# Finer steps in the norm chain, query projections packed to full tiles, and another order of copies for the latents, keys and values of the third mixer

## The reference

```python
def rmsnorm_2(x, g):
    xf = x.astype(jnp.float32)
    y = xf * lax.rsqrt(jnp.mean(xf * xf, axis=-1, keepdims=True) + RMS_EPS)
    return (y * g.astype(jnp.float32)).astype(x.dtype)
...
def mla_mixer(h, positions, w_in, q_norm_g, w_uq, kv_norm_g, w_ukv, w_o):
    q_a, kv_a, k_rope = jnp.split(h @ w_in, [Q_LORA, Q_LORA + KV_LORA], axis=-1)
    q = (rmsnorm_2(q_a, q_norm_g) @ w_uq).reshape(bsz, L, MLA_HEADS, QK_NOPE + QK_ROPE)
    q_nope, q_rope = q[..., :QK_NOPE], q[..., QK_NOPE:]
    kv = (rmsnorm_2(kv_a, kv_norm_g) @ w_ukv).reshape(bsz, L, MLA_HEADS, QK_NOPE + V_DIM)
    k_nope, v = kv[..., :QK_NOPE], kv[..., QK_NOPE:]
    q_rope = apply_rope(q_rope, cos[:, :, None], sin[:, :, None])
    k_rope = apply_rope(k_rope, cos, sin)
...
    return o @ w_o
```

## Time and profile before

| | |
|---|---|
| median of 3 runs | 1678.65 us (1676.46 to 1680.81) |
| profiled execution | 1677.19 us, span 1675.5 us, mean granted clock 0.994 |
| PE busy | 98% of the span, 14292 matmuls |
| DVE, ACT, POOL busy | 71%, 48%, 4% |
| third mixer, first query matmul to next norm's first sum | 1382.27 to 1476.31 us |

### The profile page before, as it was taken

One profiled execution on the slowest core, in us unless ns is written; L12 is line 12 of the kernel. 1 busy time (PEld: TensorE's weight loads), 2 busy tenths in 40 slices (PEclk: granted clock), 3 DMA queues, 4 the chain that ended last, 5 costly groups with the idle time before them and its releaser, 6 DMA issues.

```text
span 1675.5 us, 33931 instructions
## 1 busy us (share of the span) xinstructions
PE 1643.0 (98%) x14292; PEld 1608.0 (96%) x14292; DVE 1196.7 (71%) x1305; ACT 806.7 (48%) x870; POOL 65.7 (4%) x93
## 2 busy tenths in 40 slices
PE   9999999999999999999999999999999999999998
PEld 9999999999999999999997999999999988899997
DVE  6888876576788878888877778646545666765544
ACT  5444557654534444434565643445344555654442
POOL 0000000000000000000000000000000003200000
PEclk9999999999999999999999999999999999999999
DMA  8988744344398875988543378653455433345551
GB/s 333 352 334 307 273 176 177 127 166 162 141 350 321 321 276 212 343 325 324 201 152 126 127 265 336 221 194 155 185 200 183 168 126 128 125 169 188 197 197 54
DMA packets 50489, 365.04 MB, mean 218 GB/s; under 512 B 5728, under 2 KB 5856, under 8 KB 6240
## 3 DMA queue, kind: packets, MB, share of 16 engines
q1 hardware_dynamic: 39744, 287.04, 46.1%
q0 software_dynamic: 10368, 75.50, 12.1%
q10 hardware_dynamic: 288, 1.18, 0.2%
HBM read 362.65 MB, written 1.05 MB: 217 GB/s over the span
## 4 chain that ended last, share of the span: by engine, by line
PE 88%; DVE 7%; ACT 3%; issue 1%; DMA 0%; SPq 0%; ACTq 0%; DVEq 0%
PE bank L255 50%; PE bank L291 24%; PE bank L247 3%; PE bank L274 3%; DVE wlo L188 2%; PE bank L366 1%; PE bank L1733 1%; ACT whi L180 1%; DVE m_e L1997 1%; ACT m_e L1876 1%; PE bank L415 0%; PE bank L1691 0%; PE bank L382 0%; DMA raw<-stream_in 0%; DVE x L316 0%
## 5 line engine op out<-in xcount | busy, mean ns | idle before, releaser
L188 DVE TENSOR_TENSOR wlo<-raw,whi 128x2048 fp32r<-128x2048 f32 x261 | 597.1, 2290 | 202.5 <-ACT whi L180 201.9
L255 PE MATMUL bank<-xh,whi 128*128 128x256 f32 x2608 | 727.1, 279 | 2.5 <-DVE wlo L188 1.5
L255 PE MATMUL bank<-xl,whi 128*128 128x256 f32 x2608 | 721.3, 277 | 0.0
L255 PE MATMUL bank<-xh,wlo 128*128 128x256 f32 x2608 | 721.1, 277 | 0.0
L180 ACT ACTIVATE whi<-raw 128x2048 fp32r<-128x2048 f32 x261 | 498.3, 1913 | 306.3 <-PE bank L255 172.4
L255 PEld LDWEIGHTS bank<-xh,whi 128*128 128x128 f32 x2608 | 490.5, 188 | 4.9 <-issue 2.7
L255 PEld LDWEIGHTS bank<-xl,whi 128*128 128x128 f32 x2608 | 489.9, 188 | 0.1
L255 PEld LDWEIGHTS bank<-xh,wlo 128*128 128x128 f32 x2608 | 489.8, 188 | 0.0
L291 PE MATMUL bank<-hid_hi,whi 128*128 128x256 f32 x1056 | 292.3, 277 | 0.0
L291 PE MATMUL bank<-hid_hi,wlo 128*128 128x256 f32 x1056 | 291.9, 276 | 0.0
L291 PE MATMUL bank<-hid_lo,whi 128*128 128x256 f32 x1056 | 291.9, 276 | 0.0
(11 more groups left out here) (328 smaller groups left out, 1771.8 us busy)
## 6 DMA issues: line engine op xcount, KB each, us to landing
raw<-stream_in SPq DMA_DIRECT2D x270, 1024.0 KB, 4.8
mod_raw<-mod_in POOLq DMA_DIRECT2D x72, 1024.0 KB, 7.1
params<-params_in SPq DMA_DIRECT2D x1, 1474.0 KB, 13.9
x<-x_in SPq DMA_DIRECT2D x2, 512.0 KB, 4.4
m_gsu<-sgu_in ACTq DMA_DIRECT2D x1, 1024.0 KB, 5.0
y_out<-x SPq DMA_DIRECT2D x1, 1024.0 KB, 3.9
consts<-consts_in SPq DMA_DIRECT2D x1, 280.5 KB, 4.9
tab_pos<-pos_in ACTq DMA_DIRECT2D x1, 128.0 KB, 2.1
```

Source lines behind the costliest of these rows:

```text
L188: dve.tensor_tensor(wlo[:, s, :], raw[:, s, :], whi[:, s, :].bitcast(F32), ALU.subtract)\
L255: last = pe.matmul(out[:, m, :], (whi, wlo)[wp][:, s, k * 256 + m * P:k * 256 + m * P + P], (xh, xl)[ap][:, k, :], start=(k == 0 and j == ...
```

## The change

The norm: PE's column of ones lies in `cols`; warm-up matmuls stand 8 ahead of the second pair's sum and 2 ahead of the fourth's, where 14 stood ahead of the third's; 18 stand behind the spreading where 24 did. DVE takes the first half of the second block's low part ahead of the residual, and the second half as two quarters around the reciprocal. At the program's start the first block is loaded in two halves, the first ahead of the constants; at its end the output is stored in four pieces.

The queries: the eight blocks keep their layout in memory, but ACT and DVE write `whi` and `wlo` packed (`q_parts`): the 64 plain columns of two heads make one tile of 128, the 32 rotary columns of four heads another. Four heads (two blocks, a quad `g`) are three tiles: rotary, heads 1 and 2, heads 3 and 4; for the first quad the plain tile of block 0 comes first. A tile's 18 matmuls are three parts of 6. PE puts a head behind parts 8, 11, 14 and then behind every second part (`HEADS_BEHIND`), the swap of a quad behind parts 6, 13, 22, 31. ACT copies the plain halves to the head's slot of `m_qt` (six slots instead of four), and the rotary tile to `m_qs`; POOL multiplies it by the cosines, DVE the swapped one by the sines (`turn_q`), and DVE adds 32 rows per head (`place_q`). A split of a query block handles 1152 columns in two instructions instead of one of 2048.

Latents, keys, values: the latents of keys and values have tiles of their own (`kv_hi`, `kv_lo`, in the space of `m_o_hi`, `m_o_lo`), rounded ahead of the fourth input block's copy, their low part ahead of the value block's. ACT rounds the query latents ahead of the key copies; keys and values are copied half by ACT, half by DVE, bank by bank. POOL copies the rotated key only behind the first low part. The table preparation (`dve_tables`) fills all four groups of 32 partitions and a 128 x 128 permutation `perm4`.

```diff
-                   .then_inc(sem("w_lo_ready"), 1)
+                return
+            c0, c1 = ((H, 3 * H // 2), (3 * H // 2, BLK))[half - 1]
+            dve.wait_ge(sem("w_hi_ready"), b + 1)
+            ins = dve.tensor_tensor(wlo[:, s, c0:c1], raw[:, s, c0:c1], whi[:, s, c0:c1].bitcast(F32), ALU.subtract)
+            if half == 2:
+                ins.then_inc(sem("w_lo_ready"), 1)
 
...
 
+            dve_split_half(dve, next_stage(n), 0)
             for b, (k0, k1) in enumerate(X_TILES):
...
             if n == 0:
-                act_split_halves(act, 0)
+                act.wait_ge(sem("w_loaded_part"), 16)
+                act.activation(whi[:, 0, 0:H], raw[:, 0, 0:H], ACT.Copy).then_inc(sem("w_half_ready"), 1)
...
+            if n == 0:
+                act.wait_ge(sem("w_loaded0"), 16)
+                act.activation(whi[:, 0, H:BLK], raw[:, 0, H:BLK], ACT.Copy).then_inc(sem("w_hi_ready"), 1)
...
+        WARM_AHEAD = {1: 8, 3: 2}
...
-                    pe_keep_warm(pe, n, 14)
...
+            for t in range(N_PAIRS):
+                if t in WARM_AHEAD and n > 0:
+                    pe_keep_warm(pe, n, WARM_AHEAD[t])
+                pe.wait_ge(sem("x_paired"), N_PAIRS * pair_index[n] + t + 1)
                 for tt in range(2):
-                    mm = pe.matmul(STAT[:, T + tt:T + tt + 1], xm[:, k, tt * P:tt * P + P], ones[:, 0:1],
-                                   start=(i == 0 and tt == 0), stop=(i == len(SUMS) - 1), skip_group_check=True)
+                    mm = pe.matmul(STAT[:, T + tt:T + tt + 1], xm[:, 2 * t, tt * P:tt * P + P], cols[:, 68:69],
+                                   start=(t == 0 and tt == 0), stop=(t == N_PAIRS - 1), skip_group_check=True)
...
-            pe_keep_warm(pe, n, 10)
+            pe_keep_warm(pe, n, 15 if n == AFTER_FINAL else 10)
...
-                pe_keep_warm(pe, n, 24)
+                pe_keep_warm(pe, n, 18)
...
-            dve_split_half(dve, n, 0)
+            dve_split_half(dve, n, 1 if n else 0)
...
-            dve_split_half(dve, n, 1)
+            if n == 0:
+                dve_split_half(dve, n, 1)
+            dve_split_half(dve, n, 2)
...
+                ins = act.activation(q_parts(whi, b)[i], q_parts(raw, b)[i], ACT.Copy)
...
+                ins = dve.tensor_tensor(q_parts(wlo, b)[i], q_parts(raw, b)[i], q_parts(whi, b)[i].bitcast(F32), ALU.subtract)
...
+        Q_BANKS = (GATE, UP, STAT)
+        TILE_OF_QUAD = (0, 3, 6, 9)
+
+        def q_place(i):
+
+            return (0, (1, 0, 2)[i]) if i < 3 else divmod(i, 3)
+
+        HEADS_BEHIND = {8: 0, 11: 1, 14: 2, **{10 + 2 * h: h for h in range(3, 13)}}
+        SWAPS_BEHIND = {6: 0, 13: 1, 22: 2, 31: 3}
...
+            def q_tile(i, part):
+
+                g, r = q_place(i)
+                b = F0 + UQ0 + 2 * g
+                s0, s1 = slot_of(b), slot_of(b + 1)
+                out = Q_BANKS[i % 3][:, 0:T]
...
+                for k in (2 * part, 2 * part + 1):
+                    for p, (wp, ap) in enumerate(PASSES):
+                        w = (whi, wlo)[wp]
+                        c = k * P + (6 * P if r == 0 else 0)
+                        mm = pe.matmul(out, w[:, (s0, s0, s1)[r], c:c + P], (xh, xl)[ap][:, k, :],
+                                       start=(k == 0 and p == 0), stop=(k == 5 and p == 2))
+                if part == 2:
+                    mm.then_inc(sem("m3_tile" if i in TILE_OF_QUAD else "w_used"), 1)
...
-                    pe.wait_ge(sem("m3_q_part"), j)
-                pe.matmul(MODP[0:DQ, :], cst("rope_perm")[0:DQ, :], qs[0:DQ, j % 2].rearrange("p a t -> p (a t)"),
-                          start=True, stop=True).then_inc(sem("m3_qswap"), 1)
+                    pe.wait_ge(sem("m3_q_part"), g)
+                pe.matmul(MODP[:, 0:T], perm4[:, :], qs[:, g % 2, :], start=True, stop=True).then_inc(sem("m3_qswap"), 1)
...
-            for j in range(M3_TURNS):
-                h = 2 * (j - LAG)
-                if j < MIX3_UQ:
-                    uq(j, 0)
-                attend(h)
-                if j < MIX3_UQ:
-                    uq(j, 1)
-                    if h >= 0:
-                        attend(h + 1)
-                    swap_q(j)
-                else:
-                    out(j - MIX3_UQ, between=lambda: attend(h + 1))
-            out(MIX3_OUT - 1)
+            for c in range(3 * Q_TILES):
+                q_tile(*divmod(c, 3))
+                if c in SWAPS_BEHIND:
+                    swap_q(SWAPS_BEHIND[c])
+                if c in HEADS_BEHIND:
+                    attend(HEADS_BEHIND[c])
+            for b in range(MIX3_OUT):
+                attend(13 + 2 * b)
+                out(b, between=lambda: attend(14 + 2 * b))
...
+                if j == 3:
+                    round_latent(3)
                 act.wait_ge(sem("w_used"), F0 + j + 1)
                 if j == 0:
                     act.wait_ge(sem("m3_krope"), 1)
-                if j == 3:
-                    round_latent(3)
...
-            act_split(act, F0 + 6)
+            act_split_q(act, F0 + 6)
             root(1)
+            for b in range(3):
+                round_latent(b)
+            act_split_q(act, F0 + 7)
+            act.wait_ge(sem("m3_v_bank"), 1)
+            act.activation(v3[:, 0, 0:512], V_BANKS[0][:, :], ACT.Copy).then_inc(sem("m3_v_act"), 1)
             act.wait_ge(sem("w_used"), F0 + UKV0 + 1)
-            for q in range(4):
+            for q in range(2):
                 for r in range(2):
                     act.activation(kt[0:64, 4 * q + r:4 * q + r + 3:2, :], pair(ACC[q])[64 * r:64 * r + 64], ACT.Copy)\
                        .then_inc(sem("m3_k"), 1)
-                if q < 3:
-                    round_latent(q)
-            act.wait_ge(sem("w_used"), F0 + UKV0 + 2)
-            for i in range(2):
-                act.activation(v3[:, i, 0:512], V_BANKS[2 * i][:, :], ACT.Copy).then_inc(sem("m3_v_act"), 1)
-            act_split(act, F0 + 7)
...
+            act.wait_ge(sem("m3_v_bank"), 3)
+            act.activation(v3[:, 1, 0:512], V_BANKS[2][:, :], ACT.Copy).then_inc(sem("m3_v_act"), 1)
...
+            narrow(2)
+            read_tile(0)
+            narrow(3)
+            read_tile(1)
+            narrow(4)
+            read_tile(2)
+            behind = {0: ((read_tile, 3),), 1: ((read_tile, 4), (narrow, 5)), 3: ((read_tile, 5), (narrow, 6)),
+                      4: ((read_tile, 6),), 6: ((read_tile, 7), (narrow, 7)), 7: ((read_tile, 8),), 8: ((wide, 0),),
+                      9: ((read_tile, 9),), 10: ((read_tile, 10),), 11: ((wide, 1),), 12: ((read_tile, 11), (wide, 2)),
+                      15: ((wide, 3),), 17: ((wide, 4),)}
...
+            pool.wait_ge(sem("m3_split"), 1)
...
-            for j in range(MIX3_UQ):
...
-                    .then_inc(sem("m3_q_read"), 1)
-                pool.wait_ge(sem("m3_q_part"), j + 1)
-                pool.wait_ge(sem("m3_q_read"), j + 1)
-                pool.tensor_tensor(q, q, t1[0:DQ], ALU.add).then_inc(sem("m3_q"), 1)
+            for g in range(4):
+                pool.wait_ge(sem("m3_qs"), g + 1)
+                if g >= 1:
+                    pool.wait_ge(sem("m3_q"), 4 * g)
+                pool.tensor_tensor(t1[:, :], qs[:, g % 2, :], cos96[:, :], ALU.mult).then_inc(sem("m3_q_read"), 1)
...
+            rest(3)
             dve_split(dve, F0 + 5)
-            rest(3)
-            dve_split(dve, F0 + 6)
+            dve_split_q(dve, F0 + 6)
             scale_latent(1)
             for b in range(3):
                 rest(b)
-            for i in range(2):
-                dve.wait_ge(sem("w_used"), F0 + UKV0 + 2)
-                dve.tensor_copy(v3[:, i, 512:D], V_BANKS[2 * i + 1][:, :]).then_inc(sem("m3_v_dve"), 1)
-            dve_split(dve, F0 + 7)
...
+            dve.wait_ge(sem("m3_v_bank"), 2)
+            dve.tensor_copy(v3[:, 0, 512:D], V_BANKS[1][:, :]).then_inc(sem("m3_v_dve"), 1)
+            dve_split_q(dve, F0 + 7)
+            for q in range(2, 4):
+                for r in range(2):
+                    dve.tensor_copy(kt[0:64, 4 * q + r:4 * q + r + 3:2, :], pair(ACC[q])[64 * r:64 * r + 64])\
+                       .then_inc(sem("m3_k"), 1)
+            dve.wait_ge(sem("w_used"), F0 + UKV0 + 2)
+            dve.tensor_copy(v3[:, 1, 512:D], V_BANKS[3][:, :]).then_inc(sem("m3_v_dve"), 1)
...
+            def turn_q(g):
+
+                dve.wait_ge(sem("m3_qswap"), g + 1)
+                dve.tensor_tensor(t2[:, :], MODP[:, 0:T], sin96[:, :], ALU.mult).then_inc(sem("m3_q_part"), 1)
+                dve.wait_ge(sem("m3_q_part"), g + 1)
+                dve.wait_ge(sem("m3_q_read"), g + 1)
+
+            def place_q(h):
+
+                rows_ = slice(ROPE * (h % 4), ROPE * (h % 4) + ROPE)
+                if h >= Q_SLOTS:
+                    dve.wait_ge(sem("m3_scores"), h - Q_SLOTS + 1)
+                dve.tensor_tensor(qt[NOPE:DQ, h % Q_SLOTS, :], t1[rows_, :], t2[rows_, :], ALU.add).then_inc(sem("m3_q"), 1)
...
+            narrow(2)
```

(22 more changed lines are left out.)

228 lines of the change are left out of this document (118 added, 110 removed).

## The result

The changed kernel took 1660.83 us (median of 4 runs, 1657.6 to 1662.43), the kernel before on the same chip 1679.73 us (median of 4): ratio 0.988, 95% interval 0.986 to 0.991, 18.9 us faster. 24.7 us were forecast. The profiled execution took 1662.43 us, the longest of its four, with a span of 1660.8 us; the profiled one of before (1677.19 us) lies 2.5 us under its kernel's median. The two traces alone show 15 us, and the difference between 15 and 19 is part of what has to be explained. As a time, 1652.5 us was forecast and 1660.8 measured, which is above the forecast's own range of 1650 to 1656 and inside the wide one.

What follows compares the result with a forecast made beforehand. PE, busy 98% of the span, was taken as the bound. Terms -11.6 - 5.5 - 5.0 - 1.2 - 1.4 = -24.7 took 1677.2 to 1652.5 us; own range 1650 to 1656, wide range 1645.5 to 1662.5.

Steps and rivals of the forecast that it cites:

- Query tiles, swaps, waits: Third mixer's query stretch: 72 fewer matmuls -8.2, cheaper swaps -5.3, old waits -1.7, new waits +3.6; 94.0 to 82.4 us.
- the walk: Query stretch stepped through with row durations: new PE waits of 1.1 us at first rope swap, 1.6 us at first transpose.
- the coupling of DVE and PE: Query stretch, steady part: both need nearly equal time per head (2.9 and 3.0 us); 0.9 us of additional waits.
- the hole: Each head in the query stretch: DVE's 1 us free during ACT's exponentials, filled with one item, mostly overrun by 0.2 to 0.3 us.
- Keys, values, latents: Third mixer: PE's waits at key and value projections go, and the half clock behind the first; -5.5 us.
- Norms: Sums 0.4 us earlier, DVE's multiplies 0.65 us earlier: seven norms -4.6, the last -0.4; -5.0 us.
- D: Clock rival: 38 warm-ups in a norm instead of 48 lower PE's clock, at most 1.7 us each, +13, 1666 us; chance 0.05.
- Start: Program start: first half's copy no longer waits for the second half's load, so multiplies start earlier; -1.2 us.
- End: Program end: only the output's last quarter is behind the last multiply, landing in 2.5 instead of 3.9 us; -1.4 us.
- A: Rival in the attention chain: DVE or ACT late at every head by 0.6 us more, +9.6, 1662 us; chance 0.15.

Runs made afterwards that it cites:

- tile 1 kernel: Changed kernel with ACT's plain copies of query tile 1 moved ahead of the split of query block 3: 1660.18 us, ratio 0.988.
- old-chain kernel: Changed kernel with the norm's warm-ups, sums and split as before (14 warm-ups ahead of the third pair's sum, 24 behind the spreading): 1663.86 us, ratio 0.990.
- the one without the third mixer: Kernel before, given only the changed norm, start and end, its third mixer left as it was: 1674.54 us, ratio 0.996.
- with 12: Changed kernel with 12 warm-up matmuls in a norm instead of 38: 1668.92 us, ratio 0.993.
- with 47: Changed kernel with 47 warm-up matmuls in a norm instead of 38: 1658.61 us alone, ratio 0.988; also part of two kernels with further edits, 1653.65 and 1656.34 us.

## Why the prediction was right, and where its size was off

- **Query tiles, swaps, waits** (-11.6 forecast): 83.2 us, -10.8. The waits stood where the walk put them, 1.13 us (forecast 1.1) at the first swap and 1.54 us (1.6) at the first transpose. The step that was sized too small is the coupling of DVE and PE: the other six waits for `m_e` sum to 3.9 us, where I gave 0.9 beyond the 0.9 us that the trace of before has there. The walk had left out that DVE's item in the hole can itself be late: ahead of two of the six (0.9 and 1.0 us long), DVE waited 0.37 and 0.64 us for ACT's rounding before it could start a low part. With every pause of PE counted, idle time in the stretch went from 3.4 to 6.8 us, 3.4 us more where the forecast adds 1.9. The work fell by 14.3 us where it takes off 13.5; the query matmuls and swaps are 13.6 of that, as counted. The tile 1 kernel shows that the first wait was the split's.
- **Keys, values, latents** (-5.5): the third mixer from first projection to next norm went from 140.5 to 123.9 us, -16.6; less the query stretch that leaves -5.8. No wait and full clock at the key projection, as forecast; none of the twelve traces with the changed third mixer has a fall there, both with the old one have it.
- **Norms** (-5.0): the chain is 0.63 us shorter, 7 times, -4.4. The step that failed is the sentence by which D was put aside, "the warm-ups that go are replaced by sums that come earlier", and its chance of 0.05. The sums do come earlier, but falls came in 25 of 56 norms, 3.1 in an execution, where the old chain has 1 in 14, 0.5 in an execution. D's price of at most 1.7 us is a bound; measured is 1.1 us: 2.6 x 1.1 = +2.9 us. It gives back most of what the chain saves; the times of the old-chain kernel (0.4 us apart) and of the one without the third mixer leave open how much. The Trainium skill ("TensorE: Matmul & The Clock Gate", "What's actually happening") says that the array's clock depends on how busy the array has lately been. That spoke against taking warm-ups away, and the runs agree: falls in 7 of 7 norms with 12, in 0 of 21 with 47.
- **Start** (-1.2): the first projection starts at 13.91 instead of 14.51 us, -0.6. It varies: 13.5 to 14.7 us over the thirteen traces with the new start, so a single trace of before leaves this term uncertain by about as much as it is. ACT's second copy now stands behind the root. **End** (-1.4): from the last norm's first sum to the end 10.3 instead of 12.1 us, -1.8; the last quarter lands in 2.5 us, as taken. Other traces with the new end take up to 10.8 us.
- **Sum.** -16.6 - 4.4 - 0.6 - 1.8 = -23.4, +2.9 for the clock: -20.5, beside 18.9 and 17.6 measured, each known to about 3 us. The rest lies within that error; falls in the second mixer and the slow pitch, which were in no term, move single executions by as much. The pitch is in both kernels, and the counts don't show that the change makes it more frequent: 5 long stretches in 12 stages with the old norm chain, 22 in 48 with the finer one.
- **How right it was.** The time lies 1.7 us inside the upper end of the wide range and 4.8 us above the forecast's own, next to A's 1662, which is chance: A's chain was not late at every head. The mechanism of each main term held; the forecast took 24.7 us off, the runs show three quarters of it, and rival D, with its chance of 0.05, is the largest single part of the difference that the traces find.
